# One inference step of a convolution + latent-attention network: adaLN loads, tap waits, router stage and expert tail rearranged

## The chip, the cores and the metric

The kernel runs on one core of a Trainium2 chip. The metric is the device time of one execution in microseconds, the median of several. The engines are TensorE (PE, with its weight loads PEld), VectorE (DVE), ScalarE (ACT), GpSimd (POOL) and SyncE (SP, which issues the weight DMAs). All matrices are fp32 in DRAM.

## The reference, cut to what matters

There are 384 tokens of width 1024: 128 context tokens and 256 latent tokens. Two layers run over them. Layer 0 is a Conformer convolution (width 31, per channel) and a dense SwiGLU. Layer 1 is latent attention and a top-2-of-8 expert SwiGLU. Each sub-layer is wrapped in RMSNorm, a shift, scale and gate computed from a conditioning vector, and a residual:

```
m = silu(cond) @ ada_w + ada_b            # 6 vectors of 1024 for each layer and condition
h = rms_norm(x, g) * (1 + scale) + shift
conv:  u = a * sigmoid(g); u = conv31(u) + dw_b; u = silu(layer_norm(u)); y = u @ pw2
moe:   logits = h @ w_router; the two largest; softmax over the two -> gates
       y = sum_e gates[:, e] * (silu(h @ w1[e]) * (h @ w3[e])) @ w2[e]
x = x + gate * y
```

## The kernel before

**Weights.** SP loads every weight as a chunk of 128x2048 fp32 (1 MB) into a ring of six buffers, `raw`. An adaLN chunk is used by TensorE as it is (function `ada`), with 2 x 4 records of L1550. Any other chunk is split in two parts: ACT writes the rounded high part `wh` (`make_hi`, L248) and DVE the remainder `wl` (`make_lo`, L254), in a ring of three. Each product is then three matmuls (`mm3`, L270 to L272). So a chunk can be split only when the chunk three before it is used, and loaded when the one six before it is split or used.

**Opening.** ACT's DMA queue loads the conditioning vectors, then the tokens `x` (1.5 MB), then eleven small vector rows `vec`. SP loads the first eight adaLN chunks (n = 0 to 7); ahead of n = 3 it waits for `x`, ahead of n = 5 for `vec`. TensorE turns the vectors after n = 4 (`turn_vectors`). RMSNorm of `x`: ACT squares (L302), DVE takes the root in twelve small steps (`rsqrt`, from L278), DVE and ACT scale, TensorE transposes (L389), ACT applies scale and shift (L314), DVE splits (`split_block`, L407 and L409). `make_lo` of the first convolution chunk stands ahead of these splits.

**Convolution.** After the pointwise product, DVE does the 31 taps of six of eight channel blocks (`add_taps`, L1012, 186 instructions) and TensorE the other two by diagonal matrices (L1596), with eight adaLN chunks of layer 1 in between (one after every third matmul). DVE adds the bias of an adaLN group with `add_bias(q)` (L982), which waits for all eight chunks of the group; `add_bias(3)` stands after 24 of the 102 taps that are left then. The mean over channels comes from eight matmuls with a matrix of ones (L1612), six of them ahead of the eight gate chunks (`GATE1`). Then: centring (L1057), two `make_lo`, `add_bias(4)`, the reciprocal root (L1063), scaling, ACT's SiLU, splits, and the second pointwise product (from L270 at 217 us).

**Router stage.** After attention's last output product the residual is added for each of the three token groups of 128 (c = 0, 1, 2), then RMSNorm with twelve small DVE steps, transposes, scale and shift by ACT and DVE, 24 narrow router matmuls (L1943), transposes back to rows (L1949), the top-2 search in small DVE steps (L1363 to L1373), ranks by matmul, a 0/1 matrix `sel` by which TensorE gathers the first expert's tokens (L1969), a table of tile numbers and the weights of the last tile in further small DVE steps (L1387 to L1436), and the split of the gathered rows (L1442). Meanwhile POOL scatters all tokens into `xs_dram`, sorted by expert.

**Expert tiles.** A tile is 128 gathered tokens of one expert: six chunks each of w1, w3 and w2. The loop body does the next tile's w1 and w3 (12 chunks) and the previous tile's w2 (six), 12 matmuls of 512 columns a chunk. SiLU by ACT (L902), the product with the other half by DVE (`product`, L1452, three groups), transposes of it (`turn_hidden`, L2005), its split (`hidden_hi`, `hidden_lo`, L1458). There are eight such periods and a last w2 phase. Finally y of the earlier tiles is gathered from `ys_dram` by POOL (L638), DVE forms gate * (w_a * y_a + w_b * y_b) and adds it to `x` (`combine`, L1510 to L1514); the last tile's y stays on chip, is weighted and gated by DVE (L1520), split by ACT and DVE (L963, L1523), scattered to its tokens by TensorE with `selT` (L2061, L2062), and added (L1527).

Of the kernel before, what the change touches and what calls it, by code (L numbers as in the profile page):

```python
# [6 lines left out]
F32 = mybir.dt.float32  # L7
# [7 lines left out]
P = 128  # L15
EPS = 1e-6
# [36 lines left out]
def hybrid_conv_mla_diffusion_step(nc, d, out):  # L53
# [45 lines left out]
    POST_TAPS = (24, 60)  # L99
# [5 lines left out]
    with ctx:  # L105
# [3 lines left out]
        def share(name, *groups):  # L109

            made, most = [], 0
            for group in groups:
# [21 lines left out]
        (hTh, hTl), (ckTh, kr_rot, tq, cqTh, ckTl, cqTl), (xgh, xgl, hgh, hgl, yl) = share(  # L134
# [5 lines left out]
             ("hgh", [P, FE // P, P], F32R), ("hgl", [P, FE // P, P], F32R), ("yl", [P, D], F32R)])  # L140
# [13 lines left out]
         (hm, ms, xrow, ybuf, sel, R, rt, jt, tab, xj, js, upto, before, iota, router, rowf, rows_of,  # L154
          yh, selL, selT, gate_s, GL, slot_w, off)) = share(
# [11 lines left out]
             ("before", [P, P], F32), ("iota", [P, P], F32), ("router", [P, DK, NE], F32),  # L167
             ("rowf", [P, TC, TOP_K], F32), ("rows_of", [P, TC, TOP_K], I32),
             ("yh", [P, D], F32R), ("selL", [P, TC, P], F32), ("selT", [P, T], F32R),
             ("gate_s", [P, D], F32), ("GL", [P, TC, 2], F32), ("slot_w", [P, 2], F32), ("off", [P, TC, TOP_K], F32)])  # L170
        ps = ctx.enter_context(nc.psum_tensor("ps", [P, 8, 512], F32))
        gates_dram = nc.dram_tensor("gates_dram", [DEPTH, 2, 2, D], F32, kind="Internal").ap()
        xs_dram = nc.dram_tensor("xs_dram", [NT * P, D], F32, kind="Internal").ap()
# [114 lines left out]
        NORMS = ("conv", "ffn", "mla", "moe")  # L288
# [104 lines left out]
        MOE_BANKS = (5, 6, 7, 0, 1, 2, 3, 4)  # L393
# [29 lines left out]
        def _(sp):  # L423
# [109 lines left out]
        def _(pool):  # L533
            pool.memset(ident[:, :], 0.0).then_inc(sem("pool_steps"), 1)
            pool.memset(ones[:, :], 1.0).then_inc(sem("ones_made"), 1)
            pool.memset(epsc[:, :], EPS).then_inc(sem("ones_made"), 1)
            pool.wait_ge(sem("pool_steps"), 1)
            pool.affine_select(out=ident[:, :], in_=ident[:, :], compare_op=ALU.not_equal, fill=1.0, base=0,
                               pattern=[[-1, P]], channel_multiplier=1).then_inc(sem("ident_made"), 1)
# [41 lines left out]
            pool.wait_ge(sem("tables_blank"), 32 * NT)  # L581

# [13 lines left out]
            for i in range(2):  # L596
                for h in range(2):
# [12 lines left out]
            fetch_gate(1, 0)  # L610
            pool.wait_ge(sem("att_y"), TC * NPAIR + 1)
            pool.dma_start(router[:, :, :], d["moe_router"][0].rearrange("(k p) e -> p k e", p=P)).then_inc(sem("router_in"), 16)
# [6 lines left out]
            pool.wait_ge(sem("moe_const"), 4)  # L619
# [5 lines left out]
                               pattern=[[1, P]], channel_multiplier=-1).then_inc(sem("moe_const"), 1)  # L625
            pool.wait_ge(sem("mla_x"), TC)
# [19 lines left out]
        def _(act):  # L646
# [4 lines left out]
            act.dma_start(x[:, 0, :], d["x_prompt"][0]).then_inc(sem("x_in"), 16)  # L651
            act.dma_start(x[:, 1:3, :], d["x_sample"][0].rearrange("(c p) n -> p c n", p=P)).then_inc(sem("x_in"), 16)

# [10 lines left out]
            act.dma_start(vec[0:CW * DK - P, 2, :], taps[P:CW * DK, :]).then_inc(sem("vec_in"), 16)  # L664

# [25 lines left out]
            for i in range(PE_BLOCKS):  # L691
                for n in range(max(DIAGS, CW * i), CW * (i + 1)):
                    diagonal(n)
                act.wait_ge(sem("diag_used"), CW * (i + 1))
                act.activation(v[:, DVE_BLOCKS + i, :], ps[:, i, 0:CV], ACT.Identity,
                               bias=vT[:, DWB + DVE_BLOCKS + i:DWB + DVE_BLOCKS + i + 1]).then_inc(sem("conv_evac"), 1)
            for q in range(2):
                make_hi(act, pw2_chunk(q))
# [182 lines left out]

            norm_act(act, "moe", 1, 1, "mla_x", 0, MOE_BANKS, blocks=range(0, DK, 2))
            def token_views(c):
                return (xn[:, c, :].rearrange("p (k b a) -> p b a k", k=DK, b=DK),
                        ps[:, 2 * c:2 * c + 2, :].rearrange("p u (b a k) -> p (u b) a k", b=DK // 2, k=DK))

            for c in (0, 2):
                act.wait_ge(sem("tok_turned"), c + 1)
                act.activation(*token_views(c), ACT.Copy).then_inc(sem("tok_made"), 1)
            act.wait_ge(sem("gap_made"), 1)  # L890
            act.activation(rt[:, 9, :, 1:2], rt[:, 9, :, 0:1], ACT.Exp).then_inc(sem("gap_exp"), 1)
# [12 lines left out]
            def hidden_hi(g, loop):  # L904
# [5 lines left out]
            act.wait_ge(sem("gathered"), 1)  # L910
            act.activation(hgh[:, 0:DK, :].rearrange("p a b -> p (a b)"), ps[:, 4:6, :].rearrange("p a b -> p (a b)"),
                           ACT.Copy).then_inc(sem("xg_hi"), 1)
            make_hi(act, MOE + 2)
            for k in range(2 * UP):
                make_hi(act, MOE + k + 3)
                if k == 2:
                    act.wait_ge(sem("last_tile"), TC + 1)
                    act.activation(selT[:, :], ps[:, 6, 0:T], ACT.Copy).then_inc(sem("last_tile"), 1)
# [41 lines left out]
            for k in range(3):  # L960
                make_hi(act, NEXT + k + 3, (last, TILE_CH))
            act.wait_ge(sem("y_split"), 1)
            act.activation(yh[:, :], ybuf[:, :], ACT.Copy).then_inc(sem("y_split"), 1)  # L963
# [1142 lines left out]
```

## Time and profile before

| | |
|---|---|
| median of three runs | 1471.58 us (1470.92 to 1475.76) |
| the profiled execution | 1471.38 us, of which span 1469.6 us, so 1.8 us outside it |
| busy over the span | PE 93%, DVE 73%, ACT 51%, POOL 4% |
| moved by DMA | 349 MB, 237 GB/s over the span |
| mean granted TensorE clock | 0.975 of 2.4 GHz |

Times in rows are microseconds from the span's start. A timeline row reads: start, duration, engine, line, operation, output<-inputs, shape, count; in brackets how long the engine had been idle and what ended that. Rows of one kind that follow each other are merged, and the duration is then that of the run of them. An fp32 matmul shows as two records, a matmul of split (fp32r) parts as one. A windows row reads: stretch, its length, then busy us and (count) of PE, PEld, DVE, ACT and POOL, the granted clock, the busy share of the 16 DMA engines, and GB/s.

### The profile page before, as it was taken

The numbers are of one execution on the slowest core, as the hardware profiler recorded it, in microseconds if no ns is written. First come the engines' busy times: TensorE is split into PE (matmuls) and PEld (weight loads), VectorE is DVE, ScalarE is ACT, GpSimd is POOL, SyncE is SP. The second block draws the span as 40 slices with busy tenths as digits, with TensorE's granted clock in tenths as the row PEclk, the third lists the DMA queues.
The fourth block names the chain that finished last, engine by engine and source line by source line (L and its number), as shares of the span: only waits on it lengthen the run. The fifth ranks groups of instructions, "written<-read, shape, count | busy, mean of one in ns | idle before, by whom it ended". The sixth has DMA issues, their size and how long they took to land.

```text
span 1469.6 us, 18703 instructions
## 1 busy us (share of the span) xinstructions
PE 1370.1 (93%) x6689; PEld 1105.7 (75%) x6689; DVE 1068.4 (73%) x1347; ACT 753.1 (51%) x761; POOL 60.0 (4%) x97
## 2 busy tenths in 40 slices
PE   4999959999999989899999968999999999999986
PEld 1885527899999978677777747787887878878874
DVE  1687896534343356888888876888888888988986
ACT  2431244422221335655555533677777777777771
POOL 2000000400000001100000001000000000000001
PEclk8999989999999998999999998999999999999998
DMA  9898273994334223321222214999999999999983
GB/s 356 298 335 314 92 286 126 393 410 150 123 114 143 93 79 104 109 93 65 64 75 103 87 48 154 355 349 373 363 377 387 363 368 395 368 358 400 371 328 129
DMA packets 91017, 349.01 MB, mean 237 GB/s; under 512 B 6895, under 2 KB 43063, under 8 KB 61783
## 3 DMA queue, kind: packets, MB, share of 16 engines
q1 hardware_dynamic: 80672, 315.38, 57.8%
q0 software_dynamic: 8144, 26.52, 4.9%
q10 hardware_dynamic: 2151, 6.46, 1.1%
q8 instruction: 30, 0.49, 0.1%
q14 instruction: 20, 0.16, 0.0%
HBM read 324.01 MB, written 24.31 MB: 237 GB/s over the span
## 4 chain that ended last, share of the span: by engine, by line
PE 77%; DVE 13%; ACT 3%; issue 3%; DVEq 0%
PE ps L270 23%; PE ps L272 22%; PE ps L271 22%; DVE v L1012 3%; DVE wl L254 2%; PE ps L1550 2%; DVE hm L1452 2%; PE ps L1847 2%; PE ps L1878 1%; ACT wh L248 1%; PE ps L1596 1%; PE ps L1851 1%; PE ps L2005 1%; PE ps L389 1%; ACT QB L807 0%
## 5 line engine op out<-in xcount | busy, mean ns | idle before, releaser
L254 DVE TENSOR_TENSOR wl<-raw,wh 128x2048 fp32r<-128x2048 f32 x253 | 576.4, 2289 | 154.6 <-ACT wh L248 154.5
L248 ACT ACTIVATE wh<-raw 128x2048 fp32r<-128x2048 f32 x253 | 484.7, 1917 | 323.0 <-PE ps L272 278.7
L270 PE MATMUL ps<-wh,xgh 128*128 128x512 f32 x432 | 173.5, 402 | 0.0
L272 PE MATMUL ps<-wh,xgl 128*128 128x512 f32 x432 | 171.2, 396 | 0.0
L271 PE MATMUL ps<-wl,xgh 128*128 128x512 f32 x432 | 171.0, 396 | 0.0
L270 PE MATMUL ps<-hTh,wh 128*128 128x384 f32 x480 | 164.7, 343 | 2.1 <-DVE hTl L409 2.1
L271 PE MATMUL ps<-hTl,wh 128*128 128x384 f32 x480 | 163.3, 340 | 0.0
L272 PE MATMUL ps<-hTh,wl 128*128 128x384 f32 x480 | 163.1, 340 | 0.0
L270 PE MATMUL ps<-wh,hgh 128*128 128x512 f32 x288 | 117.5, 408 | 7.7 <-DVE hgl L1458 3.9
L271 PE MATMUL ps<-wl,hgh 128*128 128x512 f32 x288 | 115.3, 400 | 0.0
L272 PE MATMUL ps<-wh,hgl 128*128 128x512 f32 x288 | 115.2, 400 | 0.0
L1012 DVE SCALAR_TENSOR_TENSOR v<-u,dwT,v 128x399 f32<-128x399 f32 x180 | 98.9, 627 | 0.0
L270 PEld LDWEIGHTS ps<-hTh,wh 128*128 128x128 f32 x480 | 90.6, 189 | 10.8 <-issue 8.2
L272 PEld LDWEIGHTS ps<-wh,xgl 128*128 128x128 f32 x432 | 81.4, 188 | 19.8
L1090 DVE TENSOR_TENSOR ff<-ps,fs 128x384 f32<-128x384 f32 x22 | 12.3, 558 | 115.6 <-PE ps L272 115.6
L270 PEld LDWEIGHTS ps<-wh,xgh 128*128 128x128 f32 x432 | 81.4, 188 | 18.7
L271 PEld LDWEIGHTS ps<-wl,xgh 128*128 128x128 f32 x432 | 81.4, 188 | 18.3
L271 PEld LDWEIGHTS ps<-hTl,wh 128*128 128x128 f32 x480 | 90.7, 189 | 0.4
L272 PEld LDWEIGHTS ps<-hTh,wl 128*128 128x128 f32 x480 | 90.6, 189 | 0.0
L270 PEld LDWEIGHTS ps<-wh,hgh 128*128 128x128 f32 x288 | 55.0, 191 | 24.5 <-DVE wl L254 9.0
L272 PEld LDWEIGHTS ps<-wh,hgl 128*128 128x128 f32 x288 | 54.9, 191 | 13.5
L271 PEld LDWEIGHTS ps<-wl,hgh 128*128 128x128 f32 x288 | 55.1, 191 | 12.4
(339 smaller groups left out, 2091.7 us busy)
## 6 DMA issues: line engine op xcount, KB each, us to landing
raw<-in_moe_w SPq DMA_DIRECT2D x180, 1024.0 KB, 6.2
raw<-in_ada_w SPq DMA_DIRECT2D x48, 1024.0 KB, 6.7
raw<-in_ffn_w SPq DMA_DIRECT2D x33, 1024.0 KB, 6.3
raw<-in_conv_pw SPq DMA_DIRECT2D x12, 1024.0 KB, 10.8
raw<-in_mla_wo SPq DMA_DIRECT2D x8, 1024.0 KB, 4.8
xs_dram<-hf POOLq DMA_DIRECT2D x14, 512.0 KB, 20.8
ys_dram<-hf POOLq DMA_DIRECT2D x14, 512.0 KB, 21.9
raw<-in_mla_wuq SPq DMA_DIRECT2D x8, 768.0 KB, 4.5
```

Of the source, the lines that this page charges most:

```text
L248: act.activation(wh[:, split_no(s) % HL, :], raw[:, s % RAW, :], ACT.Copy).then_inc(hi_made, 1)
L254: eng.tensor_tensor(wl[:, split_no(s) % HL, :], raw[:, s % RAW, :], wh[:, split_no(s) % HL, :], ALU.subtract).then_inc(lo_made, 1)
L270: nc.tensor.matmul(out_, sh, mh, start=start, stop=False)
L271: nc.tensor.matmul(out_, sh, ml, start=False, stop=False)
L272: return nc.tensor.matmul(out_, sl, mh, start=False, stop=stop)
L389: last = pe.transpose(ps[:, banks[j], c * P:(c + 1) * P], xn[:, c, j * P:(j + 1) * P], ident[:, :])
L1012: dve.scalar_tensor_tensor(out=v[:, j, :], in0=u[:, j, w:w + CV], scalar=dwT[:, w * DK + j:w * DK + j + 1], in1=v[:, j, :], op0=ALU.mult, ...
L1452: dve.tensor_tensor(hm[:, g, :].rearrange("p (j r) -> p r j", j=4), ps[:, 3 + g, :].rearrange("p (r j) -> p r j", j=4), ms[:, g, :].rearra ...
L1550: last = pe.matmul(ps[32 * j:32 * j + 32, ADA_BANKS[q][0], :], cst[:, k, :], raw[:, s % RAW, j * 512:(j + 1) * 512], start=k == 0, stop=k ...
L1596: pe.matmul(ps[:, i, 0:CV], diag[:, m % DIAGS, :], u[:, DVE_BLOCKS + i, w:w + CV], start=w == 0, stop=w == CW - 1).then_inc(sem("diag_used ...
L1847: pe.matmul(ps[:, 2 * h + c // 2, a:b], QB[:, h, c * P:(c + 1) * P], KT[:, h, k0:k1], start=True, stop=False)
L1851: last = pe.matmul(ps[:, 2 * h + c // 2, a:b], QB[r0:r1, 2, c * P:(c + 1) * P], KR[r0:r1, k0:k1], start=False, stop=True)
```

## The change

- **Opening.** SP's two waits are gone. ACT's queue issues `vec` ahead of `x`. The vectors are turned after n = 2. DVE splits block 0 ahead of the first `make_lo`, the rest behind it.
- **Convolution.** `add_bias(3)` stands after 54 taps instead of 24; four gate chunks (`GATE_EARLY`) are put between the diagonal matmuls, one follows the mean, three follow the sums of squares; the mean's matmuls come in the order 6, 0, 1, 2, 3, 7, 4, 5; `add_bias(4)` comes after the splits; ACT makes two high parts before its last evacuation.
- **Router.** Layer 1's scale and shift vectors go, element by element, to a DRAM table `mod_rows` and back in another order (eight POOL DMAs of 1024 elements of 4 bytes), and later as rows to all partitions (`gains`, four DMAs of 0.5 MB). `x` itself is transposed; the router matrix is scaled beforehand (`routerA`), its shift part summed apart (`shifted`); the logits come from matmuls in four column groups, folded by a 0/1 matrix, and scaled by the root of each row. Tokens are scaled and shifted as rows (`token_scale`, `modulate`), so the transposes back are gone. TensorE first writes zeros with two 512-column matmuls and then gathers each token group when ready; the split of the first half of the gathered rows starts earlier. DVE's table steps are moved behind the first gathered split: some after `make_lo(MOE+2)`, some after `make_lo(MOE+3)`.
- **Expert loops.** The `k` loops begin at -1 and end one earlier, so the boundary between tiles lies one chunk earlier. The first tile's `product` is cut in its three groups, each between two `make_lo`. The last tile's weights are turned after chunk 7 instead of chunk 1.
- **End.** DVE's `combine` shrinks to one operation for each c (`own_rows`); TensorE multiplies it by a diagonal matrix of the weights (`sel`, made by ACT) in fp32 and adds the last tile in the same banks; the gate is multiplied once to the sum, then `x` is added. ACT weights the last y straight from PSUM.

The core of the diff:

```diff
-    POST_TAPS = (24, 60)
+    POST_TAPS = (24, 30, 38)
+    GATE_EARLY = 4
...
             for n in range(ADA_G):
-                if n == 3:
-                    sp.wait_ge(sem("x_in"), 32)
-                if n == 5:
-                    sp.wait_ge(sem("vec_in"), 16 * 11)
                 load_ada(n, 0, n)
...
+            for cond in range(2):
+                for i, of in enumerate((modA[:, 1, 1, cond, :], modv[:, 1, cond, 2, :])):
+                    pool.dma_start(mod_rows[0, cond, i].rearrange("(b p) -> p b", p=P), of,
+                                   allow_slow_non_contiguous=True).then_inc(sem("mod_kept"), 16)
...
-            make_lo(dve, PW1)
-            split_dve(dve, "conv", "conv_modulated", 2)
+            split_block(dve, "conv", "conv_modulated", 2, 0)
+            make_lo(dve, PW1)
+            for j in range(1, DK):
+                split_block(dve, "conv", "conv_modulated", 2, j)
...
             modulation(2)
-            add_bias(3)
             done += POST_TAPS[0]
             add_taps(done, done + POST_TAPS[1])
+            add_bias(3)
...
-                if m % 3 == 2 and n_ada < DK:
+                if m % 3 == 2 and n_ada < DK + GATE_EARLY:
...
+            modulate(1, 1)
+            modulate(2, 0)
+            modulate(2, 1)
+            make_lo(dve, MOE + 1)
+            for i in range(2):
+                dve.wait_ge(sem("token_steps"), 3 * TC + 2 + i)
+                dve.tensor_tensor(hgl[:, 4 * i:4 * i + 4, :].rearrange("p a b -> p (a b)"), ps[:, 2 + i, :],
+                                  hgh[:, 4 * i:4 * i + 4, :].rearrange("p a b -> p (a b)"), ALU.subtract).then_inc(sem("first_lo"), 1)
+            make_lo(dve, MOE + 2)
...
-                for k in range(TILE_CH):
+                for k in range(-1, TILE_CH - 1):
                     make_lo(dve, NEXT + k + 3, L)
+                    if static and k == -1:
+                        product(MOE + 2 * UP, None, 1, groups=(2,))
...
+            def own_rows(c):
+
+                dve.wait_ge(sem(f"y_back{c}"), 16 * TOP_K)
+                dve.scalar_tensor_tensor(out=yacc[:, c, :], in0=xn[:, c, :], scalar=gap[:, c, 1:2], in1=yacc[:, c, :],
+                                         op0=ALU.mult, op1=ALU.add).then_inc(sem("y_split"), 1)
...
             for c in range(TC):
+                pe.wait_ge(sem("y_split"), c + 1)
                 for h in range(2):
-                    pe.matmul(ps[:, 2 * c + h, :], selT[:, c * P:(c + 1) * P], yh[:, h * 512:(h + 1) * 512], start=True, stop=False)
+                    pe.matmul(ps[:, 2 * c + h, :], sel[:, c, :], yacc[:, c, h * 512:(h + 1) * 512], start=True, stop=False)
+                pe.wait_ge(sem("y_split"), TC + 1)
+                for h in range(2):
+                    pe.matmul(ps[:, 2 * c + h, :], selT[:, c * P:(c + 1) * P], yh[:, h * 512:(h + 1) * 512], start=False, stop=False)
```

## Rows read from the trace of the kernel before

**Rows 1.** Windows: one expert tile, and a stretch of the dense SwiGLU
```profile
1100.30:1153.40 53.10, 52.98 (x237) 42.57 (x237) 46.53 (x26) 38.97 (x25) 0.00 (x0) 1.00 0.99 384
...
340.00:380.00 40.00, 40.00 (x210) 37.49 (x210) 12.75 (x14) 9.03 (x7) 0.00 (x0) 1.00 0.40 130
```

**Rows 2.** Windows: two stretches of the opening
```profile
15.00:20.00 5.00, 0.00 (x0) 0.00 (x0) 0.00 (x0) 3.23 (x6) 0.00 (x0) 0.57 0.72 246
20.00:25.00 5.00, 4.24 (x18) 0.72 (x19) 0.00 (x0) 0.00 (x0) 0.00 (x0) 0.50 1.02 433
```

**Rows 3.** Timeline of the opening
```profile
6.69 0.45 ACTq L664 DMA_DIRECT2D vec<-in_conv_dw  x1
...
15.49 1.06 ACT L302 ACTIVATE xn<-x 128x1024 f32<-128x1024 f32 x1 [6.78 <-DMA x<-in_x_sample]
...
26.17 0.16 DVE L278 TENSOR_SCALAR nr<-st 128x3 f32<-128x3 f32 x1
...
30.21 2.15 PE L389 MATMUL ps<-ident,xn 128*128 128x128 f32 x18 [1.48 <-DVE xn L380]
...
39.29 0.67 PE L270 MATMUL ps<-hTh,wh 128*128 128x384 f32 x1
```

**Rows 4.** Timeline of DVE in the convolution
```profile
151.96 0.69 DVE L982 TENSOR_TENSOR ar<-ps,ab 128x512 f32<-128x512 f32 x1 [12.33 <-PE ps L1550]
...
185.27 15.34 DVE L1012 SCALAR_TENSOR_TENSOR v<-u,dwT,v 128x399 f32<-128x399 f32 x28
203.19 3.93 DVE L1057 SCALAR_TENSOR_TENSOR v<-ps,v 128x399 f32<-128x399 f32 x8 [2.57 <-PE ps L1612]
```

**Rows 5.** Timeline of PE in the convolution
```profile
150.82 1.07 PE L1550 MATMUL ps<-raw,cst 128*32 128x512 f32 x8
...
179.08 4.47 PE L1612 MATMUL ps<-v,ones 128*128 128x399 f32 x12
...
200.12 3.03 PE L1612 MATMUL ps<-v,ones 128*128 128x399 f32 x4 [7.05 <-DVE v L1012]
...
217.44 0.77 PE L270 MATMUL ps<-wh,hTh 128*128 128x512 f32 x1 [6.57 <-DVE hTl L409]
```

**Rows 6.** Timeline of DVE in the router stage
```profile
876.03 1.22 DVE L1311 TENSOR_TENSOR x<-x,yacc 128x1024 f32<-128x1024 f32 x1
...
893.05 0.18 DVE L1358 COPY rt<-ps 128x24 f32<-128x24 f32 x1
...
895.87 0.17 DVE L1373 TENSOR_TENSOR rt<-rt 128x3 f32<-128x3 f32 x1
...
898.73 0.16 DVE L1387 COPY jt<-ps 128x8 f32<-128x8 f32 x1
...
...
907.85 1.23 DVE L1442 TENSOR_TENSOR hgl<-ps,hgh 128x1024 fp32r<-128x1024 f32 x1
```

**Rows 7.** Timeline of PE in the router stage and at the first tile
```profile
899.02 7.25 PE L1969 MATMUL ps<-sel,xn 128*128 128x128 f32 x48 [0.77 <-ACT xn L889]
909.12 0.50 PE L270 MATMUL ps<-wh,hgh 128*128 128x512 f32 x1 [2.85 <-DVE hgl L1442]
...
951.87 0.66 PE L2005 MATMUL ps<-ident,hm 128*128 128x128 f32 x4 [2.54 <-DVE hm L1452]
```

**Rows 8.** Windows: the granted clock in the gather
```profile
900.00:905.00 5.00, 5.00 (x33) 5.00 (x33) 4.17 (x26) 0.00 (x0) 2.04 (x2) 0.68 0.20 79
```

**Rows 9.** Timeline of all engines at the end
```profile
1414.14 2.29 DVE L254 TENSOR_TENSOR wl<-raw,wh 128x2048 fp32r<-128x2048 f32 x1 [0.51 <-ACT wh L248]
...
1432.58 0.79 PE L270 MATMUL ps<-wh,hgh 128*128 128x512 f32 x1 [3.90 <-DVE hgl L1458]
...
1457.69 1.22 DVE L1523 TENSOR_TENSOR yl<-ybuf,yh 128x1024 fp32r<-128x1024 f32 x1 [1.12 <-ACT yh L963]
...
1462.72 3.48 DVE L1527 TENSOR_TENSOR x<-x,ps 128x1024 f32<-128x1024 f32 x3
```

**Rows 10.** The page: POOL's DMA queue
```profile
q0 software_dynamic: 8144, 26.52, 4.9%
```

More of the change, by code:

```diff
@@ L133, in hybrid_conv_mla_diffusion_step @@
         gate = sb("gate", [P, 2, D])
-        (hTh, hTl), (ckTh, kr_rot, tq, cqTh, ckTl, cqTl), (xgh, xgl, hgh, hgl, yl) = share(
+        ((hTh, hTl), (ckTh, kr_rot, tq, cqTh, ckTl, cqTl), (xgh, xgl, hgh, hgl, yl),
+         (_, router, routerA, routerB, shifted, fold)) = share(
             "shared24",
@@ L693, in _ @@
                     diagonal(n)
+                if i == PE_BLOCKS - 1:
+                    for q in range(2):
+                        make_hi(act, pw2_chunk(q))
                 act.wait_ge(sem("diag_used"), CW * (i + 1))
@@ L1060, in _ @@
                 make_lo(dve, pw2_chunk(q))
-            add_bias(4)
             dve.wait_ge(sem("ln_root"), 1)
@@ L1460, in hidden_lo @@
                                   ALU.subtract).then_inc(sem("hg_lo"), 1)
-            rows_lo(hgl[:, 0:DK, :], hgh[:, 0:DK, :], 4, (sem("xg_hi"), 1))
-            make_lo(dve, MOE + 2)
-            for k in range(2 * UP):
+            for k in range(1, 2 * UP - 1):
+                if k == 2 * UP - 2:
+                    product(MOE + 2 * UP, None, 1, groups=(0,))
                 make_lo(dve, MOE + k + 3)
-                if k == 2:
+                if k == UP + 1:
                     dve.wait_ge(sem("last_tile"), TC + 1)
@@ L1591, in _, with mean_of @@
             pe.wait_ge(sem("glu_done"), 8)
+            def mean_of(j, first=False, last=False):
+                if j >= DVE_BLOCKS:
+                    pe.wait_ge(sem("conv_evac"), j - DVE_BLOCKS + 1)
+                else:
+                    pe.wait_ge(sem("dve_taps"), (j // 2 + 1) * 2 * CW - 1 + j % 2)
+                return pe.matmul(ps[:, 4, 0:CV], ones[:, :], v[:, j, :], start=first, stop=last)
             n_ada = 0
@@ new lines, in _ @@
+            turn_x(0)
+            turn_x(1)
+            turn_x(2)
+            for c in range(TC):
+                pe.wait_ge(*((sem("x_kept"), 1) if c == 0 else (sem("router_made"), 4 + c)))
+                for k in range(DK):
+                    j = k % 4
+                    last = pe.matmul(ps[32 * j:32 * j + 32, R_BANKS[c], 0:P], routerA[:, 1 if c == 0 else 0, k, :],
+                                     yacc[:, c, k * P:(k + 1) * P], start=k < 4, stop=k >= 4)
+                last.then_inc(sem("router_out"), 1)
@@ new lines, in _ @@
+            pe.wait_ge(sem("router_made"), 4)
+            pe.matmul(ps[:, 5, TC * NE:(TC + 2) * NE], ones[:, :], shifted[:, :, :].rearrange("p c e -> p (c e)"), start=True, stop=True)
+            for c in range(TC):
+                pe.wait_ge(sem("router_made"), 7 + c)
+                last = pe.matmul(ps[:, 5, c * NE:(c + 1) * NE], folded[:, c, :], fold[:, :], start=True, stop=True)
+            last.then_inc(sem("logits_made"), 1)
+            pe.wait_ge(sem("moe_const"), 8)
+            for i in range(2):
+                pe.matmul(ps[:, 2 + i, :], ident[:, :], gate_s[:, 0:512], start=True, stop=False)
```

307 lines of the change are left out of this document (172 added, 135 removed).

## The prediction

> **What bounds the kernel now.** I read the chain that ended last first, then windows stage by stage, then one engine's timeline wherever PE had been idle. In an expert tile PE is busy 52.98 of 53.10 us [rows 1]; the eight periods take 53.1 us each. The dense SwiGLU is the same: 40.00 of 40.00. So neither loop can give more than about 0.1 us a period. What can move is where PE waits. Those places are six: the opening [rows 2, 3]; the taps, where DVE is the chain [rows 4, 5]; the router stage, DVE again [rows 6, 7]; the first tile's product [rows 7]; the restart after the last tile's transposes; and the combine at the end [rows 9]. I sum against the profiled execution's own 1471.4 us (span 1469.6 and 1.8 outside); the median, 1471.58, is the same for this purpose. No change that can be told from noise means within 0.3%, 4.4 us.
>
> **Opening.** DMA moved 246 GB/s from 15 to 20 us and 433 in the next 5 [rows 2]: SP stood in its waits for `x` and `vec`. Without them 187 GB/s x 5 us = 0.94 MB more is moved, 2.2 us earlier. But `x` is now queued behind `vec`. ACT issued its last `vec` row until 7.14 us, with 1.1 us of `x` issues ahead [rows 3], so `x` is issued some 4 us later and lands at 19.5 instead of 15.5; beside more weight traffic it may be 21.5. The three squares (1.06 and a 0.19 read each, 3.3 us), twelve root steps (26.17 to 28.5, 2.4 us, no longer held by the late turning of the vectors) and the scaling (1.4 us) put the transposes at 26.7 to 28.6 against 30.21 [rows 3]: a gain of 1.6 to 3.5. Splitting block 0 ahead of `make_lo` (0.9 us) is neutral, since the first product waits for both anyway. I take 2.5. Rounds of the pointwise product are PE-bound and keep it.
>
> A rule on the side. `x` came at some 120 GB/s here (1.57 MB in 13 us) beside weights at two to three times that. The Trainium skill's DMA: Bandwidth & Descriptors, section Queues, rings and completion order, says that each DMA engine takes turns between the queues that have work, packet by packet. If the turns shared evenly, `x` would land by about 15 us, and only the weights would hold the opening.
>
> **Convolution.** DVE stood 12.33 us for the adaLN bias of group 3 [rows 4], because the eight chunks are done on PE only at 151.9 [rows 5]. Thirty more taps (15.34 / 28 = 0.55 us each, 16.4 us) now cover it: the bias comes at 156, no wait. All taps end at 188.3 instead of 200.6. The wait must not turn up on PE: four gate chunks (about 1.0 us each [rows 5]) move the last diagonal matmul from 178.6 to 182.6 (plus ACT's evacuation of 0.6), and six mean matmuls (4.47 / 6 = 0.75 us) take PE to 187.1, under the 187.8 at which block 4 is done; blocks 4 and 5 then end at 189.4. Centring starts at 189.6 instead of 203.19: 13.6 us. Taking `add_bias(4)` (0.6) out from ahead of the root adds 0.1, as ACT's root is then late. Three gate chunks behind the sums of squares (3 us) lie in the 6.57 us in which PE waited for splits [rows 5]. ACT's two early high parts need chunks that are loaded once gate chunks 2 and 3 are used (161 us), long before 182. I count 13.7. PE's margin is only 0.7 us, so this term can lose: if diagonals or loads stall PE by 3 us, 2.3 of it is gone.
>
> **Router stage.** The last pair carries about ten small DVE steps more; four routerB and sum steps hide in DVE's waits, three for the fold do not: residual done 0.45 us later than 877.25 [rows 6]. From there (before's clock): transposes of `x` until 879.7, ACT's third square and root until 881, DVE's third copy out of PSUM until 882.5 (1.2 us each), one multiply 1.2, three copies 0.8, one add 1.2, three rev steps 0.6, five steps for the logits 0.9: 887.5, where the copy of the logits stood at 893.05. The thirteen small top-2 steps (2.8 us) are the same, so `gap` is at 890.4 instead of 896.0 [rows 6]: 5.6 us. Behind it DVE has a half multiply (1.25), ranks and `sel` (2.2, until 892.7), three halves (3.75, until 896.4), `make_lo` 2.3; PE gathers group by group and ends 3.5 us behind the last half, at 899.9 (24 products cost 7.25 [rows 7], 0.3 each); the first half's split is done 0.3 us later, and PE starts the first chunk at 900.4 against 909.12. That is 8.7, but not all of it stays: the table steps that stood from 898.73 to 907.8 [rows 6], 9.0 us, now lie between `make_lo` 2, 3 and 4. DVE: chunk 2 ready at 903.7, table 5.3, chunk 3 at 911.3, weights of the last tile 3.7, chunk 4 at 917.3. PE at 2.80 us a chunk (2.29 and 0.51 [rows 9]) wants chunk 3 at 908.8 and 4 at 914.1: it waits 2.5 and 3.2 us. Chunk 5 starts at 920.1 instead of 925.7: 5.6, less 0.9 for the last tile's transposes, not yet done: 4.7. After that `make_lo` is quicker than PE. The scatter is five us later, done about 918, and its first row block is wanted at 935; hidden.
> The clock: the gather ran partly at 1.2 GHz before (0.68 granted [rows 8]), and PE is now sparser ahead of it; also a 3.2 us pause stands before chunk 4, like the 2.85 after which the first chunks ran low. I take 2.0 for both (ends: 0 and, with all 24 products at 0.43 and chunk 4 low, 4.7). Leaves 2.7.
>
> **First tile.** PE stood 2.54 us for `product` behind two `make_lo` [rows 7]; in three groups between them the wait goes, and its followers just keep up (chunk 14 ready 0.4 late): 2.3 us. **Rotation:** within the loops each wait is the same, only ACT's y copy (1.0 us) comes ahead of one high part, inside a slack of over 1 us: 0.
>
> **End.** PE stood 3.90 us because a `make_hi` (1.92) and `make_lo` (2.29) went ahead of the hidden rows' split, and then ran its first matmuls at 0.63 [rows 9]. With both behind, PE restarts 2.6 earlier and stays warm (1.3): chunks end at 1446.9 instead of 1450.8. ACT's y 1.1, DVE's low part 1.3: 1449.6; before, DVE's nine combine operations (11.5 us) held this until 1458.9 [rows 9]. In fp32, 512 columns cost 0.75 x 512 / 399 = 0.96 us, so each c costs PE 1.9 and four matmuls 0.95: scattered at 1450.7, 1453.5, 1456.4; gate and add 2.5 behind the last: 1459.0 against 1466.2: 7.2. I take 6.5, the rest for POOL's gathers, for which `own_rows(0)` now waits between two splits. If PE were at 1.2 GHz here, the three rounds would take 5 us each and only 1.5 would be left.
>
> **Sum:** 2.5 + 13.7 + 2.7 + 2.3 + 6.5 = 27.7; 1471.4 - 27.7 = 1443.7; I say 1443.5.
>
> **Costed at nothing:** `gains` (2 MB) is issued at 854 and wanted at 882; the router load at 840; scaling in `routerA` in a 0.4 us gap. The eight element-wise DMAs come behind the 14 MB of zeros, about 340 us; their result is wanted at 854, and the DMA engines are 40% busy there [rows 1].
> On them the same page of the Trainium skill, section Rules for kernel authors, warns that a strided last dimension becomes one descriptor per element. No row here has such a DMA; by that rule there are 8192 element packets. It would be cover, not price, that decides.
>
> **Rivals.**
> 1. *As summed*, own range 1440 to 1448: 0.54.
> 2. *`x` shares the DMA evenly* (the rule above), then only the weights hold the opening: eight chunks and `x`, 10.1 MB at 433 GB/s [rows 2] and 2 us to start make 25.5 us, where the last of the eight was used at 32.3; the opening gains 6 instead of 2.5: 1440. For it: packets of both queues run on all engines. Against: `x` took 13 us before. 0.16.
> 3. *The router stage gives nothing back*: cold gather, or DVE's postponed table steps cost PE more pauses; router and first tile net 0: 1448.5. For it: DVE is the bound there before and after, its work is the same. 0.16.
> 4. *PE takes the taps' place or the end is cold*: 3 to 5 us lost: 1448; 0.09.
> 5. *Slower*: the element DMAs hold up the weights of the dense SwiGLU. Place: 340 to 540 us. At POOL's mean packet time (0.049 x 16 x 1469.6 / 8144 = 0.141 us [rows 10]) 8192 packets are 72 us on each of 16 engines, shared with weights that need 40%. It costs nothing until a chunk takes over six ring slots, some 45 us, and turns the result slower only past about 0.3 us a packet with the engines blocked: 1480. For it: 4-byte writes are not shown here. 0.05 with other losses of its size.
>
> Faster holds cases 1 to 4: 0.95; same 0.02; slower 0.03. The range 1438 to 1450.5 leaves out the far sides of 3, 4 and all of 5.
>
> **What would show it.** DVE idle before the bias of group 3 gone and centring at 187 (before's 189.6 less 2.5); PE's first expert chunk at 884 to 886 (900.4 less 16.2, and the clock); two PE waits of 2 to 3 us on `wl` in the first four chunks; tile period still 53.1; the last matmuls to end 9 us after the last w2 chunk, all at 0.4. Wrong it would be if `x` lands after 23 us, if the mean waits for PE, if the gather takes over 10 us, or if ACT or DVE cannot keep the pace in a tile.

## The result: faster by 1.2%, 11 us short of the forecast

The changed kernel takes 1454.62 us (median of four, 1453.64 to 1459.79), the kernel before took 1473.67 beside it (1470.92 to 1483.08): ratio 0.9878, 95% interval 0.9843 to 0.9913. Forecast were 1443.5 us and 1438 to 1450.5. Repeated later, beside eleven executions of the kernel before, the same code gave 1454.52 and 0.9872 (0.9849 to 0.9895). One of the five executions of the reordered end (told below) took 1718.95 us at a granted clock of 0.745 and is left out of its ratio.

The profiled execution of the first series was 1459.79 us, 5 us over its three neighbours; the repeat's profiled execution took 1454.61. Both profiles are used below, as "the changed kernel" and "the repeat"; where they differ (0.3 us in the opening, 0.7 in the dense SwiGLU, 1.6 in the attention, 0.5 in the router and tiles, 2.1 at the end) the repeat stands for the median. The page of the changed kernel begins like this:

```profile
span 1458.0 us, 18721 instructions
...
PE 1377.7 (94%) x6689; PEld 1104.4 (76%) x6689; DVE 1063.7 (73%) x1345; ACT 755.7 (52%) x764; POOL 78.8 (5%) x111
```

That hides everything. A ledger by stage shows it. Each mark is the start of one instruction that both kernels have: PE's ninth adaLN chunk, DVE's centring, POOL's memset for the zero tables, POOL's load of the rotary table (end of the dense SwiGLU), POOL's memset of `before` (residual of the attention done), PE's last transposes of hidden rows, and the end of DVE's last instruction. The last column is a run told below, in which one thing of the opening is put right. The 3.0 to 3.4 us behind DVE's last instruction are in the span and in no row.

| stage (us) | before | changed | repeat | `x` on SP | forecast of the change |
|---|---|---|---|---|---|
| opening, to the ninth adaLN chunk | 49.6 | 58.7 | 58.4 | 47.8 | -2.5 |
| convolution, to centring | 153.6 | 139.8 | 139.8 | 139.8 | -13.7 |
| layer norm and pw2 | 73.1 | 73.0 | 73.0 | 72.7 | 0 |
| dense SwiGLU | 273.7 | 274.5 | 273.8 | 273.4 | 0 |
| attention | 327.3 | 328.4 | 326.8 | 326.8 | 0 |
| router and expert tiles | 550.0 | 544.9 | 544.4 | 544.7 | -5.0 |
| end | 39.0 | 35.7 | 33.6 | 33.6 | -6.5 |
| span | 1469.6 | 1458.0 | 1452.8 | 1441.8 | -27.7 |

The opening lost 9.1 us where a gain of 2.5 was forecast. In the timeline of the changed kernel's opening (ACTq is ACT's DMA issue):

```profile
6.06 0.45 ACTq L684 DMA_DIRECT2D x<-in_x_prompt  x1
6.54 0.46 ACTq L685 DMA_DIRECT2D x<-in_x_sample  x1
...
18.21 0.37 PE L1621 MATMUL ps<-ident,vec 64*128 64x64 f32 x1 [4.25 <-DMA vec<-in_conv_dw]
...
28.96 1.06 ACT L308 ACTIVATE xn<-x 128x1024 f32<-128x1024 f32 x1 [20.40 <-DMA x<-in_x_sample]
...
36.27 4.07 PE L395 MATMUL ps<-ident,xn 128*128 128x128 f32 x18 [9.54 <-DVE xn L386]
...
48.29 0.69 PE L276 MATMUL ps<-hTh,wh 128*128 128x384 f32 x1
```

`x` landed at 28.96 against 15.49 before [rows 3], PE stood 9.54 us for the transposes and then ran them at low clock (4.07 us against 2.15, at 0.50 granted from 35 to 40 us), and the first product began at 48.29 against 39.29 [rows 3].

Convolution, DVE's timeline: the bias of group 3 has no wait now, where it stood 12.33 us [rows 4], and centring waits 1.24 us for PE's mean.

```profile
164.65 0.68 DVE L1025 TENSOR_TENSOR ar<-ps,ab 128x512 f32<-128x512 f32 x1
165.25 20.80 DVE L1055 SCALAR_TENSOR_TENSOR v<-u,dwT,v 128x399 f32<-128x399 f32 x38
...
198.49 3.93 DVE L1104 SCALAR_TENSOR_TENSOR v<-ps,v 128x399 f32<-128x399 f32 x8 [1.24 <-PE ps L1680]
```

Router stage, PE's timeline, to be read beside [rows 7]: gather, first expert chunk, two short waits.

```profile
890.08 8.08 PE L2053 MATMUL ps<-sel,xn 128*128 128x128 f32 x48 [1.25 <-DVE sel L1463]
...
898.68 0.50 PE L276 MATMUL ps<-wh,hgh 128*128 128x512 f32 x1
...
909.28 0.50 PE L276 MATMUL ps<-wh,hgh 128*128 128x512 f32 x1 [1.92 <-DVE wl L260]
...
914.77 0.50 PE L276 MATMUL ps<-wh,hgh 128*128 128x512 f32 x1 [2.42 <-DVE wl L260]
```

End, timelines of PE, POOL and DVE of the changed kernel, beside [rows 9]:

```profile
1422.73 0.49 PE L276 MATMUL ps<-wh,hgh 128*128 128x512 f32 x1 [1.94 <-DVE hgl L1548]
...
1425.05 2.77 POOL L660 DMA_INDIRECT yacc<-ys_dram,rows_of  x1 [509.50 <-DMA ys_dram<-ybuf]
1428.13 0.95 POOL L660 DMA_INDIRECT xn<-ys_dram,rows_of  x1 [0.30 <-issue]
1429.39 1.96 POOL L660 DMA_INDIRECT yacc<-ys_dram,rows_of  x1 [0.31 <-issue]
...
1441.83 1.28 DVE L1590 SCALAR_TENSOR_TENSOR yacc<-xn,rt,yacc 128x1024 f32<-128x1024 f32 x1 [2.72 <-DMA xn<-ys_dram,rows_of]
...
1444.36 0.50 PE L2153 MATMUL ps<-yh,selT 128*128 128x512 f32 x1 [2.35 <-DVE yl L1602]
```

PE restarts 1.94 us after its transposes instead of 3.90. POOL's issues are long, the third gather is late, DVE's low part behind it too, and PE stands 2.35 us. Windows behind the restart and behind this last wait (PE, PEld, DVE, ACT and POOL busy with counts, granted clock, DMA share, GB/s):

```profile
1422.00:1425.00 3.00, 2.27 (x10) 1.87 (x11) 2.02 (x4) 2.55 (x3) 0.00 (x0) 1.00 0.44 175
...
1444.00:1448.00 4.00, 3.64 (x7) 2.19 (x8) 2.16 (x3) 0.00 (x0) 0.00 (x0) 0.60 0.00 0
```

So here the restart keeps the 2.4 GHz level, and the last products lose it.

### The profile page after: what moved, and what is told of

Its sections match the earlier page's. It is cut to its first block, busy times and chain, and to the rows that moved or that the text cites. A ratio compares the mean times of both kernels' runs of the same rounds, so it can differ in the third digit from the quotient of the medians.

```text
span 1458.0 us, 18721 instructions
## 1 busy us (share of the span) xinstructions
PE 1377.7 (94%) x6689; PEld 1104.4 (76%) x6689; DVE 1063.7 (73%) x1345; ACT 755.7 (52%) x764; POOL 78.8 (5%) x111
## 4 chain that ended last, share of the span: by engine, by line
PE 75%; DVE 9%; DMA 4%; ACT 4%; issue 4%; POOL 1%; DVEq 0%; ACTq 0%; SPq 0%; POOLq 0%
PE ps L276 21%; PE ps L278 20%; PE ps L277 20%; DMA raw<-in_ffn_w 3%; PE ps L1686 3%; DVE wl L260 3%; PE ps L1631 2%; DVE hm L1542 2%; PE ps L1932 2%; PE ps L1963 1%; ACT wh L254 1%; PE ps L1936 1%; PE ps L2093 1%; PE ps L2053 1%; ACT QB L829 0%
## 5 line engine op out<-in xcount | busy, mean ns | idle before, releaser
L277 PEld LDWEIGHTS ps<-wl,xgh 128*128 128x128 f32 x432 | 81.4, 188 | 18.2
## 6 DMA issues: line engine op xcount, KB each, us to landing
raw<-in_ffn_w SPq DMA_DIRECT2D x33, 1024.0 KB, 10.6
```

The lines of the kernel that those rows point to most:

```text
L277: nc.tensor.matmul(out_, sh, ml, start=False, stop=False)
```

## Experiments

Ratios are to the kernel before, executed on the same chip in the same rounds. The changed kernel stands at 0.9872.

**Only the queues of the opening, in the kernel before.** `x` behind `vec`, SP's two waits gone, vectors turned after the third chunk; nothing else changed.

```diff
-                if n == 3:
-                    sp.wait_ge(sem("x_in"), 32)
-                if n == 5:
-                    sp.wait_ge(sem("vec_in"), 16 * 11)
...
-            act.dma_start(x[:, 0, :], ...)
-            act.dma_start(x[:, 1:3, :], ...)
             def vrow(n, src):
...
             act.dma_start(vec[0:CW * DK - P, 2, :], taps[P:CW * DK, :])...
+            act.dma_start(x[:, 0, :], ...)
+            act.dma_start(x[:, 1:3, :], ...)
...
-                if n == 4:
+                if n == 2:
                     turn_vectors()
```

> The kernel before with only the opening's queues changed: x behind vec, no waits on SP, vectors turned behind the third chunk. If those three edits make the loss by themselves: x lands at 28 to 29, the ninth chunk moves from 49.7 to 58 or 59, and the whole is 8 to 10 us slower than before. If the loss needs the rest of the change: within 2 us of before.

1481.22 us, ratio 1.006 (1.004 to 1.0081). `x` landed at 29.01 and the ninth chunk started at 57.6, 8.0 us late. These three edits alone make the loss.

**The same three put back in the changed kernel.**

> The changed kernel with the opening's queues and waits exactly as before: x behind the loads of c and ahead of vec, SP standing for x before the fourth chunk and for vec before the sixth, the vectors turned behind the fifth chunk. The changed arithmetic of the opening stays. If the waits and the order are the whole of the loss: x lands at 15.5, ninth adaLN chunk on PE at 49 to 50, 8.5 to 9.5 us sooner than in the changed kernel, and the whole at 1444 to 1447. If some other edit of the opening lost part of it, the ninth chunk comes at 52 or later.

1445.87 us, ratio 0.9822 (0.9808 to 0.9836). `x` at 15.34, ninth chunk at 49.71: all of the loss is back, and no gain beside it. The changed arithmetic of the opening was worth nothing with the old queues.

**Order or waits.** First try: `x` ahead of everything on ACT's queue, with SP's waits and without. My edit put `x` ahead of the two 4 KB loads of `c` as well, which the kernel before had first.

> The changed kernel with the opening's queues as before: x issued ahead of vec, SP standing for x before the fourth chunk and for vec before the sixth, the vectors turned after the fifth chunk. Theory A (x and vec came late because nothing held the weights back): x lands at 15 to 17 us instead of 28.96, the ninth adaLN chunk on PE starts at 49 to 51 instead of 58.77, and the whole is 8 to 10 us quicker than the changed kernel, 1444 to 1447. Theory B (the time went to something else in the opening, such as the root steps on DVE or the cold PE): x lands early, but PE is at the ninth chunk no sooner than 56, and the whole stays at 1452 to 1455.

> The changed kernel with x issued ahead of vec, but no waits on SP. If the order on ACT's queue is what counts: x is issued 4 us earlier and lands at about 20, PE is at the ninth chunk at 50 to 52, whole 1445 to 1448. If it is the weights at full rate that starve it: x needs about as long from issue to landing as in the changed kernel (16 and 22 us), so it lands at 24 to 25, and the whole is only 3 to 4 us better, 1450 to 1452; vec, now behind x, may then be the last.

0.9815 (0.9793 to 0.9837) and 0.9832 (0.9814 to 0.985). The larger part of `x` landed 14.4 and 14.2 us behind its issue, at 15.7 and 15.5, but `c`, 8 KB behind it, only at 16.5 and 16.7, and PE and ACT started there (ACT on `x` at 16.9 and 17.1); ninth chunk at 50.5 and 53.3. An unintended sight of the same mechanism: what stands ahead on that queue sets the time, not its own size. So once more with `c` first and no SP waits:

```diff
             act.dma_start(cnd[...], ...)
+            act.dma_start(x[:, 0, :], d["x_prompt"][0])
+            act.dma_start(x[:, 1:3, :], ...)
             def vrow(n, src):
...
-            act.dma_start(x[:, 0, :], d["x_prompt"][0])
-            act.dma_start(x[:, 1:3, :], ...)
```

> The changed kernel with x's two loads moved on ACT's queue from behind vec to ahead of it, but behind the two small loads of c (in the run x_first they were ahead of those too, and c landed only at 16.5 us behind x, so that PE began at 17). No waits on SP. Theory A (on one queue what is issued first lands first, and x needs 14 us beside full weight queues): x lands at 15.5 to 17.5, vec at 20 to 27, PE takes its first chunks from 8.7, stands for vec, and is at the ninth chunk at 49 to 53; 4 to 8 us quicker than the changed kernel. Theory B (the SP waits alone made the opening of before): ninth chunk at 56 or later.

`x` at 18.24, now `vec` last: PE stood 14.04 us for it until 28.91. Ninth chunk at 53.5, so the order is worth 4.9 us of the 8.8. The other 3.8 lie between this run and the one with all three put back; that one has SP's waits and the later turning of the vectors, and no run tells these two apart. The landing of `x` can be divided, because turning the vectors comes after it. From the issue of its larger part it took 13.2 us with SP's waits, 16.1 without them, and 21.8 behind `vec` (the repeat). So of the 13 us by which `x` came late, 4.5 are the later issue, 2.9 the missing waits and 5.7 the loads ahead of it on the queue.

The whole hardly showed it: 1453.72 us, 0.9866 (0.9842 to 0.9889), executions from 1451.13 to 1457.42. In the profiled one the stages behind centring ran at a lower granted clock. Windows (PE, PEld, DVE, ACT and POOL busy with counts, granted clock, DMA share, GB/s) of the repeat and of this run behind the centring, 5 us apart as the centrings are:

```profile
205.00:215.00 10.00, 6.35 (x34) 3.15 (x34) 9.48 (x14) 7.68 (x13) 0.00 (x0) 0.87 0.71 239
215.00:225.00 10.00, 10.00 (x44) 8.09 (x44) 8.86 (x18) 6.69 (x8) 1.07 (x2) 0.95 0.83 299
```

```profile
200.00:210.00 10.00, 6.35 (x33) 3.15 (x33) 9.47 (x14) 7.70 (x14) 0.00 (x0) 0.82 0.72 238
210.00:220.00 10.00, 10.00 (x40) 8.02 (x39) 8.55 (x17) 6.05 (x9) 1.07 (x2) 0.84 0.84 299
```

Layer norm and pw2 took 75.7 us here against 73.0, attention 328.8 against 326.8. Across its six executions the time goes with the mean granted clock, 0.984 at 1451.1 and 1451.3, 0.974 and 0.975 at 1457.1 and 1457.4 (but 0.975 at 1454.9 too). What puts one execution on one side is open.

**`x` on SP's own queue**, behind the second weight chunk, no waits.

```diff
             for n in range(ADA_G):
+                if n == 2:
+                    sp.dma_start(x[:, 0, :], d["x_prompt"][0]).then_inc(sem("x_in"), 16)
+                    sp.dma_start(x[:, 1:3, :], ...).then_inc(sem("x_in"), 16)
                 load_ada(n, 0, n)
```

> The changed kernel with x issued by SP behind its second weight chunk, on the same queue as the weights, and no waits; vec alone on ACT. If a queue is served in order and x's share of the DMA was the loss: x lands after two chunks and its own 1.57 MB at 420 GB/s, at 12 to 14 us; vec, with 130 KB on ACT's queue, still at 18 and the turned vectors behind it; PE at the ninth chunk at 46 to 50, whole 1441 to 1446. If x's landing is not the cause: 1453 to 1456.

1443.53 us (1442.68 to 1446.89), ratio 0.9784 (0.9765 to 0.9802). `x` at 13.4, ninth chunk at 47.8: 10.6 us sooner than in the repeat and 1.9 sooner than before. The span is 27.8 us under that of before; the sum had said 27.7. By medians the gain is 32.5 us, because the kernel before took 1476.06 on this chip and not 1472.65 as beside the repeat; ratios of different chips are not to be compared to a few tenths of a per cent. Its profile's opening and its first expert chunk (forecast at 884 to 886):

```profile
13.41 1.06 ACT L308 ACTIVATE xn<-x 128x1024 f32<-128x1024 f32 x1 [5.59 <-DMA x<-in_x_sample]
...
884.44 0.51 PE L276 MATMUL ps<-wh,hgh 128*128 128x512 f32 x1
```

**`x` on POOL's queue**, issued at 1.3 and 2.0 us with nothing else on it. Is it what stands ahead of `x`, or does any queue beside SP's full one get little?

> The changed kernel with x's two loads issued by POOL as its first instructions, at about 1 to 3 us, on a queue on which nothing else is then; vec alone on ACT; no waits on SP. If x was late because of what stood ahead of it on ACT's queue: x lands at 12 to 16 us, as with the SP queue, and the ninth adaLN chunk on PE starts at 47 to 50. If each queue beside SP's gets a small part of the DMA (x took 16 us from issue to landing ahead of vec): x lands at 18 to 20 us, and vec, served beside it, lands at 18 to 22; ninth chunk at 48 to 52. The whole 1443 to 1450.

1444.21 us, ratio 0.9799 (0.9777 to 0.9822). `x` at 18.3, `vec` on ACT at 21.8, ninth chunk at 48.6. So it is both: beside the weights `x` needs 16.2 us even alone on its queue, and behind `vec` it needs `vec`'s time on top.

Why a load of 0.16 MB counts is in the DMA view (packets, MB, share of 16 engines; q1 is SP's queue, q10 ACT's, q0 POOL's). From 18.2 to 22 us of the repeat, where q10 carries `x`:

```profile
q1 hardware_dynamic: 145, 1.06, 66.9%
q10 hardware_dynamic: 144, 0.53, 35.0%
```

The same stretch of `x` ahead of `vec`, where q10 carries `vec`:

```profile
q1 hardware_dynamic: 205, 1.47, 94.4%
q10 hardware_dynamic: 201, 0.08, 7.7%
```

And from 12 to 15 us of this run, with `x` on POOL's queue and `vec` on ACT's:

```profile
q1 hardware_dynamic: 111, 0.78, 63.6%
q0 software_dynamic: 108, 0.44, 36.5%
q10 hardware_dynamic: 104, 0.05, 5.7%
```

While queues have work together, they move the same number of packets, one for one, whatever is in them: some 7 KB of weights, 4 KB of `x`, 0.4 to 0.5 KB of `vec`. `c` and `vec` are 439 packets on ACT's queue in this run, with 0.17 MB, and the 1.57 MB of `x` are 416. An estimate from these rows: 439 turns of 7.3 and 0.4 KB take 8 us at the 410 GB/s moved there, and 416 turns of 7.3 and 3.7 KB take 11 us; by even bytes the 1.74 MB together would take some 8 us. The repeat's `x` landed 27.7 us after the first of these loads was issued, so some 9 us are left; the issues that went on until 7 us and POOL's 192 packets of `ab` are part of it, and how much is open.

**The bias ahead of the 30 taps.**

```diff
-            add_taps(done, done + POST_TAPS[1])
             add_bias(3)
+            add_taps(done, done + POST_TAPS[1])
```

> The changed kernel with one line moved: DVE adds the bias of adaLN group 3 ahead of its 30 taps instead of behind them; everything else of the convolution stays changed. If the 12.33 us wait is what the 30 taps cover, it returns at 11 to 12.5 us, all taps end that much later and the whole is 11 to 12 us slower, about 1466. If PE's chain of diagonals, gate chunks and means would set the end anyway, the loss is under 4 us, 1458 at most.

1468.28 us, ratio 0.9946 (0.9931 to 0.9961). In DVE's timeline the wait is back, to a hundredth:

```profile
160.38 0.69 DVE L1025 TENSOR_TENSOR ar<-ps,ab 128x512 f32<-128x512 f32 x1 [12.34 <-PE ps L1631]
```

Centring came at 211.60, the convolution took 153.5 us instead of 139.8: 12.34 of this wait, and 1.3 because DVE again stood 2.57 us for the mean, as before [rows 4], and not 1.24. The convolution's whole gain is these two waits; the expectation had left out the second.

**The modulation rows in straight order.** Contiguous stores and copies in place of the element-wise ones; this leaves the gains of the MoE rows in another order.

```diff
-                    pool.dma_start(mod_rows[0, cond, i].rearrange("(b p) -> p b", p=P), of, ...)
+                    pool.dma_start(mod_rows[0, cond, i].rearrange("(p b) -> p b", p=P), of)
...
-                                   mod_rows[0, cond, i].rearrange("(q k) -> k q", k=DK), ...)
+                                   mod_rows[0, cond, i].rearrange("(k q) -> k q", k=DK))
```

> The changed kernel with the four stores and the four DRAM-to-DRAM copies of the modulation rows in straight order (32 bytes a partition, then whole rows) instead of element by element; the gains that the MoE rows are multiplied with are then in another order, which this kernel leaves wrong, with the routing unchanged. If the element-wise DMAs hold up the dense SwiGLU's weights: the weights between 330 and 390 us land in 6 to 12 us instead of 32, and the time from the blank table to the end of the dense SwiGLU is 1 us shorter; whole 0.5 to 1.5 us quicker. If the slow weights come from the zero tables: no change.

The DMA view from 318 to 400 us, of the repeat and then of this run (count, KB each, median us to landing):

```profile
raw<-in_ffn_w SPq DMA_DIRECT2D x9, 1024.0 KB, 34.7
mod_rows<-mod_rows POOLq DMA_DIRECT2D x4, 4.0 KB, 23.0
```

```profile
raw<-in_ffn_w SPq DMA_DIRECT2D x9, 1024.0 KB, 6.0
mod_rows<-mod_rows POOLq DMA_DIRECT2D x4, 4.0 KB, 2.2
```

The weights land 29 us sooner, and it buys nothing: 0.9874 (0.9849 to 0.9898), dense SwiGLU 273.4 against 273.8 in the repeat, but 273.4 also with `x` on SP, where the element-wise DMAs stand. The expected microsecond was not there; six ring slots cover 35 us.

**The end reordered**: low part ahead of the third block's own rows, PE's own-row products of blocks 0 and 1 first.

```diff
             own_rows(1)
-            own_rows(2)
             dve.wait_ge(sem("last_tile"), TC + 3)
             dve.scalar_tensor_tensor(out=yl[:, :], ...)
+            own_rows(2)
```

> The changed kernel with two things reordered at the end: DVE makes the low part of the last tile ahead of the third block's own rows, and PE does the own-row matmuls of blocks 0 and 1 before the first that needs the low part. If the 2.72 us in which DVE stood for the third block's gather is what the low part waits for: the low part is done at 1442.7 instead of 1444.3 on the clock of the profile, PE no longer stands 2.35 us, keeps its clock, and the end is 1.5 to 2.5 us earlier. If the end is set by DVE's six last operations (7.4 us) and the third gather: 0 to 0.5.

No gain: 0.987 (0.9843 to 0.9896), end 33.8 us. In the repeat and here the third gather is back before ACT's `yh` is done (DVE waits 0.27 us for `yh` and PE 0.81 for the low part), so there was nothing to win. The 2.35 us wait belongs to another course of the end, which the profiles of four kernels show (the table below); on that one the new order was not tried.

**Low parts in four pieces.** Three of DVE's 2.29 us instructions at the end become four of 0.6 us.

```diff
+                for i in range(4):
+                    last_op = dve.tensor_tensor(wl[:, hl, i * n:(i + 1) * n], raw[...], wh[...], ALU.subtract)
+                last_op.then_inc(lo_made, 1)
```

> The changed kernel with three of the four low parts that DVE makes at the end, 2.29 us each, made in four pieces of some 0.6 us. POOL's six gathers took 0.95 us each where DVE stood idle and 1.7 to 2.8 us where they met a DVE instruction; in every such case they ended 0.8 us behind that instruction. Theory C (an issue that meets a DVE instruction stands until it ends): each gather takes at most 1.6 us, the six together 8 to 10 us with gaps instead of 11.5 to 13, DVE's third wait for a gather falls from 1.9 to 2.7 us to under 1, and the end is 0.5 to 1.5 us earlier. Theory D (the gathers are slow by their DMA queue or the other DMA traffic): durations as before.

Theory C holds for the issues. POOL's first three in this run, where the changed kernel has 2.77, 0.95 and 1.96:

```profile
1425.65 1.17 POOL L660 DMA_INDIRECT yacc<-ys_dram,rows_of  x1 [509.54 <-DMA ys_dram<-ybuf]
1427.12 1.47 POOL L660 DMA_INDIRECT xn<-ys_dram,rows_of  x1 [0.30 <-issue]
1428.90 1.07 POOL L660 DMA_INDIRECT yacc<-ys_dram,rows_of  x1 [0.30 <-issue]
```

The six end 8.4 us after the first began, not 11.5 as in the repeat, and DVE's third wait fell to 0.51. The whole did not move beyond doubt: 0.9864 (0.985 to 0.9879). Its end took 32.0 us instead of 33.6, and I first gave that to the gathers alone.

**Both together** (`x` on SP and the four pieces), and `x` on SP with the reordered end:

> x on SP's queue behind its second weight chunk (x_on_sp, 0.9784 of before), and the three low parts at the end in four pieces each (split_in_four). If POOL's issues standing behind DVE's instructions cost the end: from the last transposes of hidden rows to DVE's last instruction 31.9 to 32.4 us instead of the 33.6 of x_on_sp, whole 1 to 2 us better than x_on_sp in its profile, ratio 0.976 to 0.980. If that gain in split_in_four was the clock alone: 33.3 to 33.9.

> x on SP's queue behind its second weight chunk (as in x_on_sp, 0.9784 of before) together with the reordered end (as in end_order, which by itself gave nothing that five rounds can tell). Expected 0.976 to 0.980 of the kernel before, 1438 to 1444 us; the end's reordering is worth 0 to 1.5 us of it.

0.9777 (0.9763 to 0.979), 1443.00 us, and 0.9805 (0.9792 to 0.9817), 1444.45 us; neither is told apart from `x` on SP alone. POOL's issues were short again (all six within 8.0 us), yet the end was 33.6. So short issues by themselves bring nothing. The other half is PE's clock behind the restart: windows of split_in_four, then of the repeat and of `x` on SP with the four pieces, right behind PE's pause of 1.94 us.

```profile
1424.00:1426.00 2.00, 2.00 (x11) 1.59 (x10) 1.01 (x3) 1.15 (x1) 0.35 (x1) 1.00 0.19 72
```

```profile
1420.00:1422.00 2.00, 2.00 (x8) 1.58 (x7) 1.02 (x2) 1.45 (x1) 0.04 (x1) 0.70 0.31 123
1422.00:1425.00 3.00, 3.00 (x10) 2.37 (x9) 1.86 (x1) 0.82 (x1) 2.72 (x1) 0.63 0.02 5
```

```profile
1411.00:1414.00 3.00, 3.00 (x10) 2.34 (x10) 1.76 (x3) 1.30 (x1) 2.39 (x3) 0.64 0.44 117
```

The 14 profiles with the new end fall into four groups (the two with the reordered end, 33.7 and 33.8, stand with the repeat's):

| clock behind the restart | POOL's issues long | low parts in four pieces |
|---|---|---|
| falls to about 0.6 | end 33.6 to 33.8 (the repeat, `x` on SP and six others) | 33.6 (one profile) |
| stays at 1.00 | end 35.7 to 35.9 (changed kernel, `x` ahead of `vec`, `x` ahead of all with SP's waits, modulation rows in order) | 32.0 (one profile) |

A PE that stays quick is no gain by itself. It is through with w2 sooner, two more of POOL's issues meet a DVE instruction (six in 11.5 to 12.9 us), the third gather is 2.3 to 3.1 us late, PE stands 2.35 to 2.87 us for the low part, and its last products then run at about 0.6. Only with short issues too did the quick restart shorten the end. That corner rests on one execution.

**The changed kernel again**, as a neighbour for these runs:

> The changed kernel once more, unedited, on the chip of the runs beside it, so that they have a direct neighbour. Expected 0.985 to 0.990 of the kernel before. Its profiled execution of the first series was 5 us longer than its three others; if that was an accident of one execution, this one's span lies at 1452 to 1454 and the opening still has x landing at 28 to 29 us and the ninth adaLN chunk on PE at 58 to 59.

It held: span 1452.8, `x` at 28.46, ninth chunk at 58.4.

## Why the prediction failed, and where it held

**Opening: the step that failed.** "So `x` is issued some 4 us later and lands at 19.5 instead of 15.5; beside more weight traffic it may be 21.5." It landed at 28.5 to 29. The step priced the later issue (4 us; it was 4.5) and took the time from issue to landing over from the kernel before, with 2 us at most for more weight traffic. That time rose from 13 us to 21.8: by 2.9 because SP no longer stood (from 12 to 15 us ACT's queue moved 549 packets in the kernel before, where SP's moved 21, and 135 in the repeat), and by 5.7 because `vec` was ahead, which the step priced at nothing. `vec` is small in bytes, 0.16 MB, but with `c` it is 439 packets, as many as `x`. The forecast's own sign of failure, "if `x` lands after 23 us", is what happened. The term is +8.8 to +9.1 instead of -2.5; that is 11.3 to 11.6 us, and the span missed the sum by 10.9 in the repeat.

**The 27.8 for 27.7 is in part luck.** In the run with `x` on SP's queue the opening gained 1.9 by another way than the forecast's 2.5, the end 5.4 instead of 6.5, and 1.5 came from stages and a tail costed at nothing. The terms of the convolution, the router and the end stand by their stage marks, and not by this total.

**Rival 2, even shares**, had the rule right and the unit wrong. Its working gave `x` half of the bytes, and `x` landed far behind its 15 us. The Trainium skill's DMA: Bandwidth & Descriptors, section Queues, rings and completion order, says that the turns between queues go packet by packet. The trace agrees: 145 and 144, 205 and 201 packets in the same stretch, at three quite different sizes. `x` then gets a third of the bytes beside the weights, and `vec` is not small.

**Convolution**: 13.7 forecast, 13.8 measured, in every run. DVE waits 1.24 us for PE's mean at centring, where the working has 1.3 between the last tap (188.3) and centring (189.6), and the layer norm behind took no more.

**Router and first tile**: 5.0 forecast, 5.1 to 5.6 measured. In the first profile the first chunk starts 10.4 us earlier; 2.8 of it were there when the stage began, so the stage gave 7.7 up to there, where the forecast was 8.7 less the clock. Waits 1.92 and 2.42 where 2.5 and 3.2 were worked out, gather 7.7 to 8.1 us; the 2.54 us wait for the first tile's `product` is gone. The parts were not tried one by one. Rival 3 is out. **Rotation**: nothing, as said; it was not tried by itself.

**Dense SwiGLU**: rival 5's mechanism exists, its price is 0.1 us in the repeat (0.8 in the first profile, which was longer in most stages). Weights that took 6 us took 35 beside element-wise DMAs. The forecast put the cover at some 45 us, and 35 us a chunk cost nothing.

**End**: 6.5 forecast, 5.4 in the repeat, 3.3 in the first profile. "PE restarts 2.6 earlier" came as 1.96 earlier, and "stays warm" held in five of the 14 profiles only. Where it held with long issues, the cold came at the last products instead, and the end lost 3.2 of the forecast's 6.5, which is rival 4's cold end at its price; where it did not, 1.1. The working had 0.7 for POOL's gathers and no price for issues that stand behind DVE's instructions; these make the third gather 1.6 to 1.9 us late in the one course, mostly under the wait for `yh`, and 2.3 to 3.1 in the other, where nothing hides it.

## What to carry to other kernels

Before a load is moved behind others on a side queue, count the packets ahead of it, not the bytes: eleven loads of short rows were as many packets as 1.5 MB. A wait that only seems to hold a queue back may be what gives another queue the DMA; if it is to go, put the urgent load on the full queue itself, at its place in the order. And take the landing time of a transfer from a stretch with the same neighbours, or not at all.

## What the runs showed of the hardware

- Queues that had work at the same time moved equal numbers of packets: 145 and 144, 205 and 201, and with three queues 111, 108 and 104, at some 7, 4 and 0.4 KB a packet. Beside SP's full queue ACT's moved 38 packets a microsecond with `x` (144 in 3.8 us) and 53 with `vec` (201), and 183 where SP's stood (549 in 3 us). On SP's own queue the same 1.57 MB landed 11.2 us behind the issue of its larger part, with two chunks ahead of it.
- POOL's indirect DMA issue takes 0.95 us, and 1.4 to 2.8 when it begins while DVE is in a long instruction; it ended 0.8 to 0.9 us behind that instruction's end (1427.82 behind 1426.96, 1433.79 behind 1432.98, and five more in the two profiles). An issue that began 0.3 us ahead of such an instruction took 0.94 (1426.28 against 1426.59 in the repeat). With DVE's work in 0.6 us pieces no issue at the end took over 1.47. The Trainium skill's SBUF — State Buffer, section SBUF: two separate sides, has such a lock: a DVE instruction with two SBUF inputs holds the port pair that it shares with POOL against a POOL operation that reads SBUF, and whichever starts first has it for the whole instruction. The long DVE instructions here have two SBUF inputs, and the issue reads its row numbers from `rows_of`. The trace agrees for POOL: it waited where it came second, and not where it came first.
- Executions of one kernel lie up to 11 us apart with the same instructions (1478.60 to 1489.34 for the kernel before with the new queues), and in most the longer time has the lower mean granted clock (there 0.972 and 0.962). A stage's clock behind a pause of PE is not fixed: after the same pause of 1.94 to 1.99 us at the end it stayed at 1.00, the 2.4 GHz level, in five profiles, and fell to about 0.6, a mixture with 1.2 GHz, in nine. Differences under 2 us between single profiles were read here from stage marks, not from spans.
